# Four layer norm tiles inside two attention heads, a regrouped first merge chunk and an earlier load of output weights

## The reference

```python
h = rmsnorm(x, rms_g) * (1 + scale) + shift
q, k, v, z_a, glu, z_b, gates = jnp.split(h @ w_in + b_in, PROJ_SPLITS, axis=-1)
y_a = attend(q, k, v) * jax.nn.silu(z_a)             # 8 heads of 64
y_b = silu(layernorm(depthwise_conv(a * sigmoid(b)))) * jax.nn.silu(z_b)
g_a, g_b = jnp.split(jax.nn.sigmoid(gates), 2, axis=-1)
m = g_a * (y_a @ w_proj_a) + g_b * (y_b @ w_proj_b)
return x + gate * (m @ w_out), k, v
```

## Time and profile before

| What | Value |
|---|---|
| Median of the three runs | 1966.09 us |
| The profiled execution, its own time | 1966.39 us |
| Its span, first to last instruction | 1964.6 us |
| Mean granted TensorE clock | 0.990 |
| Busy share TensorE, VectorE, ScalarE, GpSimd | 97%, 52%, 27%, 6% |
| DMA moved | 235.06 MB, 120 GB/s in the mean |
| Attention, merge, output begin at | 1166, 1517, 1749 us |

### The profile page before, as it was taken

How to read it: one execution, slowest core, us unless ns; L and a number is a source line. 1 busy time by engine, 2 the same in 40 slices (tenths; PEclk the granted TensorE clock), 3 DMA queues, 4 the chain that set the end, 5 groups by cost and what they waited for, 6 DMA issues and landing times.

```text
span 1964.6 us, 26940 instructions
## 1 busy us (share of the span) xinstructions
PE 1909.1 (97%) x10707; PEld 1641.6 (84%) x10707; DVE 1022.9 (52%) x1619; ACT 534.7 (27%) x1109; POOL 125.2 (6%) x225
## 2 busy tenths in 40 slices
PE   7999999999999999999999989999989899999998
PEld 1788899988888888888888879999988878887886
DVE  2544512121388178538817955666647655554443
ACT  2641101011111111111101125555657322222221
POOL 0000000000000000000000031232220000001000
PEclk9999999999999999999999999999999999999999
DMA  8514413232122022212211449776654656663421
GB/s 281 184 62 163 149 65 132 80 130 86 33 78 78 33 68 84 70 32 78 77 34 53 121 129 199 134 165 156 138 126 137 210 185 200 191 218 113 163 99 54
DMA packets 206999, 235.06 MB, mean 120 GB/s; under 512 B 46379, under 2 KB 155803, under 8 KB 202779
## 3 DMA queue, kind: packets, MB, share of 16 engines
q1 hardware_dynamic: 206616, 233.23, 40.1%
q10 hardware_dynamic: 259, 0.11, 0.0%
HBM read 152.52 MB, written 80.78 MB: 119 GB/s over the span
## 4 chain that ended last, share of the span: by engine, by line
PE 93%; ACT 2%; DVE 1%; SPq 1%; issue 1%; DMA 1%; POOL 0%; POOLq 0%; ACTq 0%; DVEq 0%
PE banks L759 17%; PE banks L760 16%; PE banks L761 16%; PE banks L1123 5%; PE banks L1623 3%; PE banks L1624 3%; PE banks L1625 3%; PE banks L1125 3%; PE banks L1592 3%; PE banks L1594 3%; PE banks L1593 3%; PE banks L1101 2%; PE banks L754 2%; PE banks L755 2%; PE banks L756 2%; PE banks L1106 2%
## 5 line engine op out<-in xcount | busy, mean ns | idle before, releaser
L759 PE MATMUL banks<-h_hi,w_hi 128*128 128x512 f32 (+1 forms) x1600 | 593.8, 371 | 2.9 <-DVE w_lo L544 1.8
L760 PE MATMUL banks<-h_lo,w_hi 128*128 128x512 f32 (+1 forms) x1600 | 589.8, 369 | 0.0
L761 PE MATMUL banks<-h_hi,w_lo 128*128 128x512 f32 (+1 forms) x1600 | 589.7, 369 | 0.0
L700 DVE SCALAR_TENSOR_TENSOR conv_acc<-glu_out,taps,conv_acc 128x773 f32<-128x773 f32 x360 | 371.9, 1033 | 12.3
L759 PEld LDWEIGHTS banks<-h_hi,w_hi 128*128 128x128 f32 x1600 | 302.2, 189 | 56.4 <-DVE w_lo L544 2.7
L761 PEld LDWEIGHTS banks<-h_hi,w_lo 128*128 128x128 f32 x1600 | 302.0, 189 | 50.8
L760 PEld LDWEIGHTS banks<-h_lo,w_hi 128*128 128x128 f32 x1600 | 302.3, 189 | 49.2
L484 ACT ACTIVATE out_stage<-banks,param_cols 128x512 f32<-128x512 f32 (+1 forms) x120 | 77.0, 647 | 442.4 <-PE banks L761 436.5
L1158 DVE CUSTOM_DVE_ANT_0 scores<-banks,bias 128x640 f32<-128x640 f32 (+2 forms) x128 | 106.5, 833 | 65.2 <-PE banks L1087 63.7
L1592 PE MATMUL banks<-y_hi,wp_hi 128*128 128x512 f32 (+1 forms) x320 | 123.2, 385 | 3.8 <-DVE y_lo L1763 2.9
L1593 PE MATMUL banks<-y_lo,wp_hi 128*128 128x512 f32 (+1 forms) x320 | 120.9, 378 | 0.0
(11 more groups left out here) (156 smaller groups left out, 2495.4 us busy)
## 6 DMA issues: line engine op xcount, KB each, us to landing
proj<-out_stage SPq DMA_DIRECT2D x96, 256.0 KB, 2.0
w_raw<-in_w_in SPq DMA_DIRECT2D x44, 512.0 KB, 4.0
gates_in<-proj SPq DMA_DIRECT2D x64, 256.0 KB, 3.1
k_hi<-k_hi_rows SPq DMA_DIRECT2D x16, 640.0 KB, 11.4
k_lo<-k_lo_rows SPq DMA_DIRECT2D x16, 640.0 KB, 13.9
w_ada<-in_w_ada SPq DMA_DIRECT2D x8, 1024.0 KB, 11.2
x_rows<-in_x_sample SPq DMA_DIRECT2D x4, 2048.0 KB, 11.4
x_out<-in_x_sample SPq DMA_DIRECT2D x16, 512.0 KB, 3.5
```

The lines of the kernel that those rows point to most:

```text
L700: op = dve.scalar_tensor_tensor(dst, src, tap, dst, ALU.mult, ALU.add)
L759: pe.matmul(out, w_hi[:, s, k], h_hi[c][:, k], start=first, stop=False)
L760: pe.matmul(out, w_hi[:, s, k], h_lo[c][:, k], start=False, stop=False)
L761: op = pe.matmul(out, w_lo[:, s, k], h_hi[c][:, k], start=False, stop=last)
```

## The change

1. Four tiles of layer norm are done inside attention, two from iteration 10 of head 2 and two from iteration 10 of head 4 (PAIR_AT), and GpSimd does their roots right after the bias tables of heads 3 and 5. Each pair has a buffer of its own (cv_pair), and a SiLU of its own after the last exponent. The turn_out of the next head pair waits for the pair before it.
2. The first merge chunk takes its units in the order of M_UNITS: blocks in pairs, both a units and then both b units. The conv half is wanted at unit 2. Only tiles 4 and 5 are turned there: in after units 4 and 9, back after units 8 and 13. The product, high and low half of tiles 2 and 3 are made there at units 0 to 2. SyncE loads the second z_b pair and the gates of two blocks first.
3. w_proj lies as [P, block o, k-block, 128].
4. Output weights of half 1 are loaded once eight units of merge chunk 4 are done, into the place of blocks 0 to 3 of w_proj, and split in that chunk (WO_AT). The output units take both halves of a tile from the start. Buffers of w_out and the merged rows are placed anew.
5. load_v(0) moves from part 2 of the first loads to part 1.

```diff
@@ first loads, turn_out, GpSimd
             if part == 1:
                 load_window(q, 0)
+                load_v(0)
...
-        if gg == GROUPS * (HEADS // 2 - 1):
-            pe.wait_ge(tail_stage.lin_done, 2)
+        if gg in (GROUPS, 2 * GROUPS):
+            pe.wait_ge(tail_stage.lin_done, 2 * gg // GROUPS)
...
-        tail_stage.early_pool(pool)
         for n in range(1, HEADS):
             bias_tables(n)
+            if n in (3, 5):
+                tail_stage.early_pool(pool, [n - 3, n - 2])
@@ constants, buffers
-OUT_UNITS = [(p, h) for h in range(2) for p in range(4)] + [(p, h) for p in range(4, NTOK) for h in range(2)]
+OUT_UNITS = [(p, h) for p in range(NTOK) for h in range(2)]
+M_UNITS = [(0, o, b) for e in range(0, 8, 2) for o, b in ((e, 0), (e + 1, 0), (e, 1), (e + 1, 1))]
+M_UNITS += [(c, o, b) for c in range(1, 5) for o in range(8) for b in range(2)]
-EARLY_LN = TPH * 6 + 7
+PAIR_AT = [TPH * 2 + 10, TPH * 4 + 10]
-    wp_hi, wp_lo, wp_raw = split_pair("wp", [P, 8, D], 0)
+    wp_hi, wp_lo, wp_raw = split_pair("wp", [P, 8, 8, P], 0)
-    for h, where in enumerate((X_AT, 0)):
-        wo_hi[h], wo_lo[h], wo_raw[h] = split_pair(f"wo{h}", [P, KC, 512], where)
+    for h, where in enumerate((X_AT, X_AT + 16384, X_AT + 16384, 32768, 0, 0)):
+        kind, dtype = (("hi", F32R), ("lo", F32R), ("raw", F32))[h % 3]
+        (wo_hi, wo_lo, wo_raw)[h % 3][h // 3] = at(f"wo{h // 3}_{kind}", [P, KC, 512], where, dtype)
+    for c, hi_at, lo_at in ((4, F0, ln_at), (0, 49152, 57344), (1, Y_AT, Y_AT + 16384), (2, F0, ln_at), (3, 16384, 49152)):
...
+    def turns(c):
+        j = [(2, 4, 8), (3, 9, 13)] if c == 0 else [(i, 1 + 3 * i, 4 + 3 * i) for i in range(4)]
+        return [(first_tile(c + 1) + i, a, b) for i, a, b in j] if c < 4 else []
@@ SyncE
     def tail_sync(sp):
-        for og in range(3):
+        for og in range(2):
             load_gates(sp, og)
-        for lt in (2, 3):
-            load_cv(sp, lt)
-            load_zb(sp, lt)
+        load_cv(sp, 4)
+        load_zb_pair(sp, 1)
+        load_gates(sp, 2)
+        load_cv(sp, 5)
         io.store_last_y(sp)
         load_ya(sp, 1)
+        load_zb(sp, 4)
+        load_zb(sp, 5)
...
+            if c == 4 and o == 4:
+                sp.wait_ge(mm, 72)
+                for p in range(4, 8):
+                    load_wo(sp, p)
...
-        sp.wait_ge(mm, 80)
-        load_wo(sp, 4)
-        load_wo(sp, 5)
@@ TensorE
+        for n, (c, o, branch) in enumerate(M_UNITS):
+            s, w = n % 16, MC[c][1]
+            if s == 0:
+                pe.wait_ge(ya_lod, 2 * c + 2)
+            if s == (1 if c else 2):
+                pe.wait_ge(yb_lod, yb_count(last_tile(c)))
...
+                pe.matmul(out, wp_hi[:, o, kk], y_hi[c][:, kk], start=(k == 0), stop=False)
@@ ScalarE
-            dst = cv0[:, b, P * lt:P * lt + P] if lt < 2 else act_sb[:, lt % 2, b]
-            op = act.activation(dst, src, ACT.Identity if lt < 2 else ACT.Silu, ...
+            dst = cv_pair[lt // 2][:, b, P * (lt % 2):P * (lt % 2) + P] if lt < 4 else act_sb[:, lt % 2, b]
+            op = act.activation(dst, src, ACT.Identity if lt < 4 else ACT.Silu, ...
+    WO_AT = [3, 5, 6, 7, 10, 12, 13, 14]
...
+            if c == 4 and s in WO_AT:
+                wo_high(act, WO_AT.index(s))
...
-            if i < 4:
-                wo_high(act, 4 + i)
@@ VectorE, one unit: gate it, then
+            if n == 0:
+                gate_yb(dve, 2)
+            if n == 2:
+                yb_low(dve, 2)
+            for lt, a, b in turns(c):
+                if s == b + 2:
+                    yb_low(dve, lt)
+                if s == b + 1:
+                    gate_yb(dve, lt)
+                if s == a:
+                    stats_of(dve, lt)
+                    shift_of(dve, lt)
...
+            if c == 4 and s - 1 in WO_AT:
+                wo_low(dve, WO_AT.index(s - 1))
@@ inside attention
+    def pair_steps(m):
+        return [(lt, m - PAIR_AT[lt // 2] - 5 * (lt % 2)) for lt in range(4)]
...
+            silu_pair(act, 0)
+            silu_pair(act, 1)
```

More of the change, by code:

```diff
@@ L1356, in tail @@
     f = F0 + 2 * 8 * 256 * 4
-    zb0, cv0, normed0 = at("zb_first", [P, 4, 256], f), at("cv_first", [P, 4, 256], f + 4096), at("normed_first", [P, WB], f + 8192)
+    zb0, normed0 = at("zb_first", [P, 4, 256], f), at("normed_first", [P, WB], F0 + 4096)
+    cv_pair = [at(f"cv_pair{e}", [P, 4, 256], f + 4096 + 4096 * e) for e in range(2)]
     stats = F0 + 28672
@@ new lines, in tail_pe @@
+        for n, (c, o, branch) in enumerate(M_UNITS):
[4 more added lines that the diff above has]
+                pe.wait_ge(yb_lod, yb_count(last_tile(c)))
+            if c == 0:
+                pe.wait_ge(wp_lod, o + 1)
+            if n >= 6:
+                pe.wait_ge(g_done, n - 5)
+            else:
+                io.wait_bank(pe, RING[n])
+            out = banks[:, RING[n % 6], 0:w]
+            for k in range(4):
+                kk = 4 * branch + k
+                pe.matmul(out, wp_hi[:, o, kk], y_hi[c][:, kk], start=(k == 0), stop=False)
+                pe.matmul(out, wp_hi[:, o, kk], y_lo[c][:, kk], start=False, stop=False)
+                last = pe.matmul(out, wp_lo[:, o, kk], y_hi[c][:, kk], start=False, stop=(k == 3))
+            last.then_inc(mm, 1)
+            if n == 1:
+                io.last_turn(pe)
+            for lt, a, b in turns(c):
+                if s == b:
+                    turn_back(pe, lt)
+            for lt, a, b in turns(c):
+                if s == a:
+                    turn_in(pe, lt)
@@ L1869, in ln_rstd @@
         pool.tensor_tensor(rstd[:, lt % 2], var_eps[:, lt % 2], half[:], ALU.pow).then_inc(rs_done, 1)
-    def early_pool(pool):
-        pool.memset(half[:], -0.5).then_inc(half_set, 1)
-        pool.memset(half2[:], -0.5).then_inc(half_set, 1)
-        pool.wait_ge(half_set, 2)
     def tail_pool(pool):
-        for lt in range(NTOK):
+        for lt in range(4, NTOK):
             ln_rstd(pool, lt)
@@ L1912, in early_act @@
     def early_act(act, m):
-        for lt in range(2):
-            if m == EARLY_LN + 5 * lt + 2:
+        for lt, d in pair_steps(m):
+            if d == 2:
                 norm(act, lt)
-            if m == EARLY_LN + 5 * lt + 4:
+            if d == 4:
                 back(act, lt)
@@ L1924, in early_act, with early_pool @@
         if m == NT - 1:
-            silu_first(act)
+            silu_pair(act, 0)
+            silu_pair(act, 1)
         if m == NT:
             yb_high(act, 0)
+    def early_pool(pool, lts):
+        if 0 in lts:
+            pool.memset(half[:], -0.5).then_inc(half_set, 1)
+            pool.memset(half2[:], -0.5).then_inc(half_set, 1)
+            pool.wait_ge(half_set, 2)
+        for lt in lts:
+            ln_rstd(pool, lt)
     T.sync, T.pe, T.act, T.dve, T.pool = tail_sync, tail_pe, tail_act, tail_dve, tail_pool
```

312 lines of the change are left out of this document (130 added, 182 removed).

## The result

The changed kernel takes **2004.08 us** (median of four executions, 1999.68 to 2006.28), the kernel before 1965.57 beside it: ratio 1.0188, with a 95% interval of 1.0163 to 1.0213. It is 38.5 us slower; the forecast was 1952. The profiled execution took 2003.73 us for a span of 2002.1.

The account below looks back on a forecast made before the run. TensorE, busy 97% of the span, plus the holes in it were taken to bound the kernel. Gains 6.2 + 2 + 0 + 6.2 + 0 = 14.4 us gave 1966.39 - 14.4 - 0.3 = 1951.7, said as 1952; range 1943 to 1959.

Parts of the forecast that it names:

- the slower case: Heads 2 and 4: GpSimd's tables end after the statistics, delaying the root; 1975 us with 12 us of lateness; chance 0.03.
- (a): Whole kernel: the forecast itself holds, 1952 us; chance 0.55.
- (b): First merge chunk: bound by TensorE as stores land in 2 us; gain 8 and not 2, 1946 us; chance 0.17.
- (d): First merge chunk: slower stores, five waits 1 us longer each, half clock behind holes; costs 3, 1957 us; chance 0.10.
- (f): Merge: matmuls run at another pace with the new weight addresses; 4.6 us, 1947 us; chance 0.08.
- (c): Output stage: second-half weights still late, hole moves from output unit 4 to 1; gain 0, 1958 us; chance 0.07.
- signs of being right: Trace: no TensorE hole over 1 us in heads 2, 4, 6; head 6 about 41 us; no output-stage hole, among others.
- Part 1, layer norm inside attention: Attention: head 6's excess of 12.0 us goes, two pairs cost 5.8; gain 6.2 us (1.6 to 8.4).
- Part 2, the first merge chunk: Merge chunk 0: VectorE and the stores set its end; gain 2 us, bounds 8 and -3.
- Part 3, weights block by block: w_proj layout: VectorE passes and DMA runs cost the same in both layouts; 0 us, or the pace rival.
- Part 4, output weights: Output stage: hole of 4.54 us and 1.7 of half speed behind it go; gain 6.2 us.
- Part 5, load_v(0): First loads, before attention: TensorE is busy for all of 131 us in either place; 0, bounds -1 and +1.

Follow-up runs that it names:

- e1: Changed kernel with conv and z_b loads of each chunk's third and fourth tile (chunks 1 to 3) due two tiles earlier, as in the kernel before: 1952.84 us, ratio 0.9928.
- e2: Kernel before with only those conv and z_b loads made due at their own tile's turn, as in the changed kernel: 2018.93 us, ratio 1.0267.
- e3: Changed kernel with only the conv loads put back to the earlier due time, z_b loads left late: 1968.52 us, ratio 1.0008.
- e4: Changed kernel with only the z_b loads put back to the earlier due time, conv loads left late: 1988.52 us, ratio 1.0111.
- e6: e1 with the layer norm pairs at index 7 of heads 2 and 4 and not index 10: 1975.70 us, ratio 1.0050.
- e5: Kernel before with its two early layer norm tiles starting at index 10 of head 6 and not at 7: 1957.03 us, ratio 0.9951.
- e8: e1 with the 1 MB y_a load and two z_b loads issued behind the stores of the first two sums, not ahead: 1950.00 us, ratio 0.9919.
- e10: e1 with the output stage undone: weight blocks 4 to 7 loaded behind the last merge unit, split between output units, old unit order: 1961.97 us, ratio 0.9978.
- e7: e1 with the first merge chunk's units in plain order (tile, then half), not pairs of like halves: 1950.01 us, ratio 0.9920.
- e11: e1 with edits of e7 and e8, first merge layer norm tile turned in after unit 3, next chunk's conv loads one round earlier: 1949.26 us, ratio 0.9913.
- e12: As e11, but with the pairs of like halves kept in the first merge chunk: 1948.90 us, ratio 0.9910.

## Why the prediction was wrong

**The step that failed** is not a term of the sum but one that it lacks. Its first step says that the change moves work between queues, "so its worth is read there", in the holes of the kernel before. So chunks 1 to 3, which had nearly no hole, were taken as unchanged. The front text says that SyncE's order is that of its program, and the prediction costed SyncE's new order only around chunk 0. The due times inside the loop over the sums, `turn_in_after(c)[j - 2]` against `a`, were not compared, and their cost was put at nothing without a reason. The runs showed 51.2 us in its place when the due times were mended (e1) and 53.3 when they were put into the kernel before (e2), 35.7 of it by conv rows and 15.7 by z_b rows (e3, e4). An estimate from rows was within reach: the merge stores landed 2.1 to 5.1 us after their issue. Six conv loads that land as they do, each wanted at the moment of its issue, would cost 13 to 31 us of TensorE, before half clock and before z_b.

Nor was it among the rivals. All of them were about steps that the argument had looked at. A kernel 38.5 us slower stood outside the range, and the slower case had a chance of 0.03. Its chances are also added up wrongly: (a), (b), (d) and (f) alone make 0.90, which with most of the 0.07 of (c) is more than the 0.91 given. Most of its signs of being right came true all the same (head 6 took 40.64 us, heads 2 and 4 had no hole, nor had the output stage), because these looked only at stages that the sum costed.

**Part 1, layer norm inside attention: 6.2 forecast, 4.4 measured, 5.6 without head 0.** Head 6 gave back 12.0 us, as worked out from the earlier trace rows. The pairs cost 3.08 and 3.04 us against 2.9. Attention's stretch is only 4.4 shorter, because head 0 was 1.2 us longer: its 333 matmuls are busy for 41.8 us and not 40.5, at a granted clock of 0.93 and not 0.96. The roots in heads 2 and 4 came as soon as the tables had ended, and VectorE waited 0.98 and 1.32 us for them (forecast 1.4). e6 confirms the tolerance of 2.1 us and the wait as the mechanism. What the prediction did not say is that the gain comes from the place inside the head and not from the choice of heads: index 10 in the old head 6 gives 10.2 us there and takes 1.5 in the next (e5).

**Part 2, the first merge chunk: 2 forecast, 1.2 measured, and nothing with the next chunk.** The chain was right in kind: VectorE waited 6.0 us in front of gate 4 (forecast 4.4), TensorE had a hole of 3.8 before the first turn back (forecast about 3) and one of 2.8 before the first unit of chunk 1, where VectorE sets the end as forecast, and the store was late since it was queued behind the y_a and z_b loads (e8). The term that was short is the landing: 8.0 us from the y_a issue was forecast, 9.5 measured in e1 (1518.96 to 1528.46). The hole of 2.90 us at the second unit went, but 2.0 us of it stand before the last attention turn instead. The 1.2 us are no firm figure: chunk 0 took 38.2 to 39.9 us in the six profiles with this program (after, e1, e3, e4, e6, e10), and 39.3 to 40.0 in three with the old one (before, e2, e5). The gain itself is gone when chunk 1 is added: 90.5 us in e1 against 89.7, though two tiles fewer are turned. That the first unit of chunk 1 came 8.8 us earlier in the span, where some 8 were forecast, is luck: 3.2 of them are the earlier start of attention. The new order gains nothing: in plain order the two chunks take 2.3 us less (e7), and beside the other edits 0.5 less (e11 against e12). By the Trainium skill (DMA: Bandwidth & Descriptors, section Anatomy of one DMA, given there for GpSimd's queue) a store of 128 KB takes 2.3 us, an estimate from its fixed cost and rate. That fits e8, where nothing large stands ahead of the store and it took 2.2 us, and not e1, where 1.5 MB do and it took 6.7.

**Part 3, weights block by block: 0 forecast.** A merge unit of 512 columns has its matmuls start 0.23 us apart in both profiles, and chunk 4 takes 45.0 and 45.1 us. The rival of another pace did not come true.

**Part 4, output weights: 6.2 forecast, 6.4 measured,** and 6.3 when undone (e10). No output unit of the changed kernel waits for weights.

**Part 5, load_v(0): 0 forecast.** TensorE is busy for all of the 131 us up to attention, as in the earlier trace rows:

```profile
1033.00:1164.00 131.00, 131.00 (x661) 112.03 (x660) 102.67 (x100) 20.77 (x31) 15.79 (x23) 1.00 0.38 99
```

This part was not run alone. Attention began between 1167.3 and 1168.4 us in the three kernels with the old place and between 1165.1 and 1168.7 in the eleven with the new one, so a gain of the order of its bound of 1 us is not excluded. The 3.2 us between the profiles before and after are all there at 100 us of the span, long before either place.

With the loop mended (e1) the kernel takes 1952.84 us where the sum said 1952. That agreement is partly luck. In its ledger against the profile before, attention is 5.8 us shorter, chunks 0 and 1 together 0.8 longer, chunks 2 and 3 0.8 longer and the output 6.4 shorter, and 2.4 us come from an earlier start of attention, which no edit explains. Without that start the stages give 10.5 us and not the 14.4 of the sum.

## What to carry to other kernels

When a table of due times is rewritten, check each user of it and not only the stages that the change is about. A load has to be due when its buffer comes free, and not at the moment its data is wanted. In a diff, cost every line that moves a DMA issue, those of renaming above all, by the pair issue time and first use in the timeline. A small store that frees a buffer is late behind large loads on its queue (6.7 us against 2.2 here), but moving it pays only until the next store meets the same loads. Work that has to wait for a third engine is first shifted to where that engine is free in the same period, before it is moved to another.

## What the runs showed of the hardware that was not expected

The same hole does not always cost the same clock. Head 0 of attention is the same work in all these kernels, with a hole of 3.7 to 3.9 us of TensorE near its start. It took 45.2 us in seven profiled executions, 46.0 to 46.6 in four and 48.4 to 48.5 in three, at different granted clocks. Windows over head 0 and over the 10 us behind its hole, in e1:

```profile
1165.90:1211.10 45.20, 40.50 (x333) 39.76 (x334) 21.52 (x50) 23.55 (x67) 12.08 (x23) 0.96 0.88 195
1173.20:1183.20 10.00, 10.00 (x71) 9.80 (x72) 4.16 (x9) 4.38 (x13) 9.92 (x19) 0.83 1.02 219
```

and in e10:

```profile
1166.30:1214.75 48.45, 43.73 (x333) 42.87 (x334) 21.54 (x50) 23.69 (x67) 12.08 (x23) 0.89 0.79 183
1173.60:1183.60 10.00, 9.99 (x46) 9.78 (x46) 2.64 (x6) 2.90 (x8) 9.92 (x19) 0.51 1.03 223
```

The hole is 3.77 us long in e1 and 3.78 in e10. Behind it TensorE has the high level (2.4 GHz) for about two thirds of the 10 us in e1 and for nearly none of them in e10, and 71 matmuls run there against 46. Over the head the same 333 matmuls are busy for 3.2 us longer.

By the Trainium skill (TensorE: Matmul & The Clock Gate, Part 1) the number of slow matmuls of one kernel differs from run to run. The windows agree, and here it is 3.2 us of one stage.

Attention's start came between 1165.1 and 1168.7 us, and head 1 began between 1210.8 and 1216.9 in the fourteen profiles, up to 6 us apart. e1 and e10, which are one program to that point, reach the first merge unit 4.0 us apart. That is as much as a whole part of the change, so an edit of less is read from its own stretch of the trace.
